# Up-projection of a streaming-encoder block by seven half-size products instead of eight (one level of Strassen's scheme), one core

## The reference, cut to what matters

```python
def conv_gated_mlp(h, w_up, conv_w, conv_b, w_down):      # h (2048, 1024), w_up (1024, 5632)
    z = causal_depthwise_conv(h @ w_up, conv_w, conv_b)   # 3 taps along the tokens, per column
    g, val = jnp.split(z, 2, axis=-1)                     # 2816 gate columns, 2816 value columns
    return (jax.nn.gelu(g, approximate=False) * val) @ w_down
```

## Time and profile before

| | us |
|---|---|
| median of 3 runs (1 core) | 2282.29 |
| lowest, highest | 2281.48, 2282.68 |
| span of the profiled execution | 2280.0 |
| input projection, 0 to 369 | 369.0 |
| mixer, 369 to 791.4 | 422.4 |
| up-projection, 791.4 to 1768.5 | 977.1 |
| down-projection, 1768.5 to 2280 | 511.5 |

### The profile page before, as it was taken

One profiled execution on the slowest core, in us unless ns is written; L12 is line 12 of the kernel. 1 busy time (PEld: TensorE's weight loads), 2 busy tenths in 40 slices (PEclk: granted clock), 3 DMA queues, 4 the chain that ended last, 5 costly groups with the idle time before them and its releaser, 6 DMA issues. The chain is left out here.

```text
span 2280.0 us, 25840 instructions
## 1 busy us (share of the span) xinstructions
PE 2111.2 (93%) x9568; PEld 1717.9 (75%) x9568; DVE 1169.0 (51%) x1238; ACT 632.4 (28%) x912; POOL 481.3 (21%) x317
## 2 busy tenths in 40 slices
PE   4999995789889599999999999999999799999997
PEld 3788884566666378888888888888887588888886
DVE  8698983688888444434424334334344311144333
ACT  4555552344444232221121121121121300031110
POOL 5488773243443200000000000000000000002333
PEclk9999997799999799999999999999999899999999
DMA  6310125223333242112111111111210622342220
GB/s 236 138 43 35 60 74 163 64 91 108 98 100 103 96 149 74 37 37 74 37 37 58 53 37 41 70 37 37 74 37 35 224 76 87 115 134 86 76 87 37
DMA packets 125599, 185.54 MB, mean 81 GB/s; under 512 B 7361, under 2 KB 90305, under 8 KB 122305
## 3 DMA queue, kind: packets, MB, share of 16 engines
q1 hardware_dynamic: 99616, 149.31, 20.1%
q10 hardware_dynamic: 25952, 35.86, 4.4%
HBM read 117.90 MB, written 67.24 MB: 81 GB/s over the span
## 5 line engine op out<-in xcount | busy, mean ns | idle before, releaser
L1387 PE MATMUL u_mm<-u_hT_hi,u_w_hi 128*128 128x512 f32 x1408 | 549.1, 390 | 15.4 <-DVE u_hT_lo L1355 15.4
L1387 PE MATMUL u_mm<-u_hT_lo,u_w_hi 128*128 128x512 f32 x1408 | 548.8, 390 | 0.0
L1387 PE MATMUL u_mm<-u_hT_hi,u_w_lo 128*128 128x512 f32 x1408 | 548.7, 390 | 0.0
L1501 POOL TENSOR_TENSOR d_total<-d_total,d_g 128x1024 f32 x16 | 38.2, 2387 | 1406.1 <-DVE d_total L1588 1406.1
L1321 DVE TENSOR_SCALAR u_y<-u_z,u_taps,u_bias 128x2048 f32<-128x2048 f32 x43 | 57.9, 1347 | 529.9 <-ACT u_z L1269 529.9
L1387 PEld LDWEIGHTS u_mm<-u_hT_hi,u_w_hi 128*128 128x128 f32 x1408 | 265.0, 188 | 70.6 <-DVE u_hT_lo L1355 15.8
L1269 ACT COPY u_z<-u_mm 128x512 f32<-128x512 f32 x176 | 103.2, 587 | 748.8 <-PE u_mm L1387 748.8
L1387 PEld LDWEIGHTS u_mm<-u_hT_hi,u_w_lo 128*128 128x128 f32 x1408 | 265.1, 188 | 55.2
L1387 PEld LDWEIGHTS u_mm<-u_hT_lo,u_w_hi 128*128 128x128 f32 x1408 | 265.1, 188 | 55.1
L1625 PE MATMUL d_y<-d_wd_hi,d_a_hi 128*128 128x512 f32 x704 | 218.9, 392 | 20.7 <-DVE d_wd_lo L1560 20.5
L1625 PE MATMUL d_y<-d_wd_hi,d_a_lo 128*128 128x512 f32 x704 | 217.8, 390 | 0.0
(11 more groups left out here) (172 smaller groups left out, 2506.9 us busy)
## 6 DMA issues: line engine op xcount, KB each, us to landing
u_w_raw<-w_up SPq DMA_DIRECT2D x44, 512.0 KB, 5.8
d_a_raw<-gated_scr SPq DMA_DIRECT2D x32, 704.0 KB, 5.3
gated_scr<-u_y SPq DMA_DIRECT2D x21, 1024.0 KB, 4.6
d_wd_raw<-w_down SPq DMA_DIRECT2D x22, 512.0 KB, 4.7
a_xs<-x SPq DMA_DIRECT2D x16, 512.0 KB, 4.7
m_h_in<-h_scr SPq DMA_DIRECT2D x16, 512.0 KB, 3.4
h_scr<-m_r ACTq DMA_DIRECT2D x16, 512.0 KB, 4.0
h1T_scr<-m_h1T ACTq DMA_DIRECT2D x16, 512.0 KB, 4.4
```

The lines of the kernel that those rows point to most:

```text
L1387: last = nc.tensor.matmul(mm[m][n][:], w[:, m, k, :], h[:, k, bass.ts(n, BLK)], start=(k == 0 and w is w_hi and h is hT_hi), stop=(k == KT ...
L1501: nc.gpsimd.tensor_tensor(tile_of(t), tile_of(t), g_bc[:], ALU.mult).then_inc(scaled_ok, 1)
```

## The change

Three things change in `phase_up`.

**Seven products for eight.** The activations are taken as a 2 x 2 matrix of blocks, by feature half (tiles 0 to 3, tiles 4 to 7) and by token half, the weights of a pair as a 2 x 2 matrix by column tile (gate, value) and feature half. Winograd's form of the scheme gets the four output blocks from seven products of half-size operands, named P1 to P7. Four of the seven weight operands are sums of blocks (`w_sum`: 128x512 each, made by POOL for every pair as `sum1` to `sum4`), four of the seven activation operands are sums too (`t1` to `t4`, once a pass, DVE and POOL). Each operand of a product, 7 on either side, is split into `hi` and `lo` as before. The products are 4 x 3 matmuls of 128x512. P2 is added to P1 in bank 0, P4 to P7 in bank 2, P3 to P5 in bank 3; DVE forms the sums `u2 = P1 + P6`, `u3 = u2 + P7`, and from them the blocks c22, c21 and c12, each from one tile in SBUF and one bank in PSUM (128x512); c11 is P1 + P2, copied by ACT. P4 waits until u3 has read bank 2, P3 until c22 has read bank 3.

**Two passes.** Tokens go in two passes of 1024 with all 22 pairs in each: 44 steps of 7 products. The weights are loaded twice (1 MB for a pair). The last two columns of `z` of each pair are kept in `edge` for the second pass. The activation operands have one set of buffers, which the second pass overwrites in the steps `turn` (21) and `again` (22).

**Moved work.** The first tap with the bias goes from DVE (`tensor_scalar`) to ACT (`activation` Identity with scale and bias), over 1024 columns; the product of gelu and value goes to POOL, except in the last step. Banks are read by DVE, where before ACT copied them all. The last step is no longer cut into pieces of 512 tokens.

In `phase_project` the allocations are closed before its end and its semaphores are cleared by POOL, since the new phase needs more of them.

The core of the diff:

```diff
@@ phase_project
+        ctx.pop_all().close()
+        nums = sorted(s.num for s in used)
+        assert nums == list(range(nums[0], nums[-1] + 1))
+        nc.gpsimd.sem_clear(range(nums[0], nums[-1] + 1))
@@
+P1, P6, P7, P5, P4, P3, P2 = range(7)
+STD = (P1, P6, P7, P5, P4, P3, P2)
+OPEN0 = (P1, P2, P5, P6, P7, P3, P4)
+OPEN1 = (P1, P5, P6, P7, P3, P2, P4)
+BANK = {P1: 0, P2: 0, P6: 1, P7: 2, P4: 2, P5: 3, P3: 3}
+FRESH = (P1, P6, P7, P5)
@@ phase_up: PE
+            def product(st, s, order, fresh):
+                pe.wait_ge(wlo_ok, 7 * st.i + STD.index(s) + 1)
+                if fresh is not None:
+                    pe.wait_ge(rlo_ok, 7 * fresh + RLO[fresh].index(s) + 1)
+                if s in FRESH and not (isinstance(st.i, int) and st.i < 2):
+                    pe.wait_ge({P1: c11_ok, P6: u2_ok, P7: c21_ok, P5: c12_ok}[s], st.i - 1)
+                if s not in FRESH:
+                    pe.wait_ge({P2: p1_ok, P4: u3_ok, P3: c22_ok}[s], st.i + 1)
+                for k in range(HK):
+                    for w, h in ((w_hi, r_hi), (w_hi, r_lo), (w_lo, r_hi)):
+                        last = nc.tensor.matmul(mm[st.slot][BANK[s]][:], w[:, s, k, :], h[:, s, k, :],
...
+                last.then_inc(mm_ok, 1)
@@ phase_up: DVE
+            def make_u3(st, order):
+                dve.wait_ge(mm_ok, made(st, order, P7))
+                dve.wait_ge(u2_ok, st.i + 1)
+                nc.vector.tensor_tensor(u3[:], u2[:], mm[st.slot][2][:], ALU.add).then_inc(u3_ok, 1)
...
+            def step(st):
+                nxt = st.plus(1)
+                if st.p:
+                    pad(st)
+                make_u2(st, STD)
+                weights_lo(nxt, P1)
+                weights_lo(nxt, P6)
+                make_u3(st, STD)
+                weights_lo(nxt, P7)
+                make_c22(st, STD)
+                weights_lo(nxt, P5)
+                make_c21(st, STD)
+                weights_lo(nxt, P4)
+                convolve(st, 1)
+                make_c12(st, STD)
+                weights_lo(nxt, P3)
+                weights_lo(nxt, P2)
+                convolve(st, 0)
+                if not st.p:
+                    keep_edge(st)
@@ phase_up: POOL
+            def sum1(st):
+                pool.wait_ge(w_ld[st.slot], 16 * st.half + 16)
+                if not (isinstance(st.i, int) and st.i == 0):
+                    pool.wait_ge(wlo_ok, 7 * st.i - 7 + P3 + 1)
+                nc.gpsimd.tensor_tensor(w_sum[:, 0, :, :], w_raw[:, st.slot, 1, 0:HK, :], raw_of(st, P4), ALU.add).then_inc(s_ok, 1)
...
+            def gate(st):
+                pool.wait_ge(gelu_ok, st.i + 1)
+                pool.wait_ge(convv_ok, st.i + 1)
+                nc.gpsimd.tensor_tensor(y[:, 1, :], y[:, 1, :], y[:, 0, :], ALU.mult).then_inc(act_ok, 1)
...
+            def step(st):
+                gate(st.plus(-1))
+                sum4(st.plus(1))
+                sums(st.plus(2))
@@ phase_up: ACT
+            def step(st):
+                nxt = st.plus(1)
+                keep_p1(st, STD)
+                weights_hi(nxt, P1, STD)
+                gelu(st.plus(-1))
+                for s in (P6, P7, P5, P4):
+                    weights_hi(nxt, s, STD)
+                tap_v(st)
+                weights_hi(nxt, P3, STD)
+                take_c11(st, STD)
+                weights_hi(nxt, P2, STD)
+                tap_g(st)
@@ phase_up: SP
+            def step(st):
+                refill(st, st.j + 2)
+                store(st.plus(-1))
@@ phase_up: the first step of a pass, DVE
+            def first(st):
+                nxt = st.plus(1)
+                weights_lo(st, P1)
+                right_lo(0, P1)
+                for s in (P6, P7, P5):
+                    weights_lo(st, s)
+                right_lo(0, P2)
+                weights_lo(st, P4)
...
+                nc.vector.tensor_tensor(stage[:, 1, :, :], stage[:, 1, :, :], stage[:, 0, :, :], ALU.subtract).then_inc(t1_ok, 1)
+                weights_lo(st, P3)
+                weights_lo(st, P2)
+                right_lo(0, P5)
+                right_lo(0, P3)
+                right_t2(0)
...
+                right_lo(0, P6)
+                right_lo(0, P7)
+                make_u2(st, OPEN0)
+                weights_lo(nxt, P1)
+                right_lo(0, P4)
+                make_u3(st, OPEN0)
```

More of the change, by code:

```diff
@@ new lines, in steps @@
+        def steps(eng, step, first, turn, again, final):
+            first(Step(0, 0, 0))
+            step(Step(0, 1, 0))
+            with eng.Fori(1, FT // 2 - 1) as n:
+                step(Step(n, 0, 0))
+                step(Step(n, 1, 0))
+            step(Step(FT // 2 - 1, 0, 0))
+            turn(Step(FT // 2 - 1, 1, 0))
+            again(Step(FT // 2, 0, 1))
+            with eng.Fori(FT // 2, FT - 1) as n:
+                step(Step(n, 1, 1))
+                step(Step(n, 2, 1))
+            final(Step(FT - 1, 1, 1))
@@ L1243, in store @@
[L1243 to L1251, removed]
@@ new lines, in penultimate, with turn, again, final @@
+            def penultimate(st):
+                step(st)
+            def turn(st):
+                refill(st, 1)
+                store(st.plus(-1))
+                sp.wait_ge(rlo_ok, 7 + RLO[1].index(P5) + 1)
+                sp.wait_ge(t2_ok, 2)
+                load_b(stage[:, 1, :, :], 1, 1, 0, b21_ld)
+            def again(st):
+                refill(st, 2)
+                store(Step(FT // 2 - 1, 1, 0))
+            def final(st):
+                store(st.plus(-1))
+                store(st)
+                sp.wait_ge(act_st, 16 * 2 * FT)
@@ new lines, in _ @@
+            first(Step(0, 0, 0))
+            step(Step(0, 1, 0))
+            with sp.Fori(1, FT // 2 - 1) as n:
+                step(Step(n, 0, 0))
+                step(Step(n, 1, 0))
+            refill(Step(FT // 2 - 1, 0, 0), 0)
+            store(Step(FT // 2 - 2, 1, 0))
+            turn(Step(FT // 2 - 1, 1, 0))
+            again(Step(FT // 2, 0, 1))
+            with sp.Fori(FT // 2, FT - 2) as n:
+                step(Step(n, 1, 1))
+                step(Step(n, 2, 1))
+            step(Step(FT - 2, 1, 1))
@@ new lines, in final @@
+            def final(st):
+                gate(st.plus(-1))
+            first(Step(0, 0, 0))
+            step(Step(0, 1, 0))
+            with pool.Fori(1, FT // 2 - 1) as n:
+                step(Step(n, 0, 0))
+                step(Step(n, 1, 0))
+            step(Step(FT // 2 - 1, 0, 0))
+            turn(Step(FT // 2 - 1, 1, 0))
+            again(Step(FT // 2, 0, 1))
+            with pool.Fori(FT // 2, FT - 2) as n:
+                step(Step(n, 1, 1))
+                step(Step(n, 2, 1))
@@ new lines, in take_c11, with tap_last @@
+            def take_c11(st, order):
+                act.wait_ge(mm_ok, made(st, order, P2))
+                nc.scalar.copy(z[:, 0, PAD:PAD + BLK], mm[st.slot][0][:]).then_inc(c11_ok, 1)
+            def tap_last(st, m):
+                s = bass.ds(2 * st.j + m, 1)
+                nc.scalar.activation(y[:, m, :], z[:, m, PAD:], ACT.Identity, bias=bias[:, s],
+                                     scale=taps[:, s, PAD:PAD + 1].rearrange("p o t -> p (o t)")).then_inc(tapv_ok if m else tapg_ok, 1)
@@ L1410, in phase_down, with step, first, again @@
+            def step(st):
+                for s in STD:
+                    product(st, s, STD, None)
+            def first(st):
+                for s in OPEN0:
+                    product(st, s, OPEN0, 0)
+            def again(st):
+                for s in OPEN1:
+                    product(st, s, OPEN1, 1)
+            steps(pe, step, first, step, again, step)
 def phase_down(nc, w_down, ln_g, ln_b, act_scr, h1_scr, out):
```

487 lines of the change are left out of this document (335 added, 152 removed).

## The result

The changed kernel takes 2317.41 us (median of 4 runs, 2314.94 to 2319.28) where the kernel before takes 2282.07 on the same chip (4 runs, 2281.48 to 2282.68): 1.0154 times as long, interval 1.0139 to 1.0168. It is slower by 35 us; forecast were 13 us less. The profiled executions span 2312.8 and 2280.0 us.

A forecast was written before the change was run, and what follows sets the result against it. PE bounds the up-projection; afterwards steady steps take 20.0 us with the port. Opening, steps, turn and end sum to a phase end of 1755.7 against 1768.5, 12.8 us less: 2269.5 from 2282.29, range 2228 to 2304.

The forecast's parts named there:

- Products removed: PE in the up-projection: 528 fewer matmuls, 3696 left, worth 119.6 us at most; 19.03 us a step.
- The common port: DVE instructions with two SBUF inputs and POOL's SBUF reads exclude each other; four waits, some 4 us a step.
- Rival A: Steady steps: the port hardly binds, POOL falls into DVE's idle; 19.0 to 19.5 us a step, 2204 to 2258; chance 0.20.
- The steady step: One u3 to the next with port waits: 20.0 us, PE standing about 1 us before P4.
- the ring: Loop through DVE, ACT, one product of PE and four waits for POOL, back to the next u3: 20.0 us.
- Rival B: From c21 to the next u3: DVE sets the time, slower from 20.3 us a step; 2281 to 2312, chance 0.31.
- The second pass: Steps after the turn between passes: 20 steps at 20.0 us each, as in the first pass.
- the walk: The engines' queues followed in order from the start of u3 through one steady step, giving 20.0 us.
- The clock: PE's stop of about 1 us a step before P4 is too short to lower its clock.
- Opening, turn and end: Step 0 ends at 848.4; steps 21 to 23 take 24.0, 44.5 and 24.1 us; after the last product 10.6 us.
- Rival C: ACT reloads tables between Identity and Gelu, 1.28 us each: ring above 21, time 2330; chance 0.04 with anything above.
- The range: Whole kernel's time, 2228 to 2304 us, leaving out half of Rival A and the top tenth.

The follow-up runs named there:

- e1: Changed kernel with POOL's gate product replaced by a memset that only writes, in 43 of the 44 steps; 2230.28 us.
- e4: Changed kernel with the product of gelu and value moved from POOL to DVE, directly behind u3, nothing left out; 2233.35 us, 0.9789 of the kernel before.
- e10: e4 with POOL's three 2048-wide subtractions (t4, t1, t3) moved to DVE; 2224.92 us, 0.9753 of the kernel before.
- e11: e10 with the low parts of P6's and P7's activations made ahead of the first pass's last tap sums; 2221.43 us, 0.9737 of the kernel before.
- e6: Changed kernel with taps and bias read at a constant address on ACT and DVE instead of one from the loop's register; 2290.49 us.
- e5: Changed kernel without the 4-column copy at the start of the second pass's steady steps; 2299.69 us.
- e7: Changed kernel with a 4-column copy like the second pass's added to the first pass's steady steps; 2325.89 us.
- e9: e7 with a second such copy and a wait for its end, just ahead of u3 in the first pass; 2338.64 us.

## Why the prediction was wrong

By its own sum, from the phase's start, in us:

| | forecast | measured | |
|---|---|---|---|
| to the end of step 0 | 57.0 | 57.4 | +0.4 |
| step 1 | 24.1 | 26.9 | +2.8 |
| steps 2 to 20 | 380.0 | 391.4 | +11.4 |
| steps 21 to 23 | 92.6 | 96.9 | +4.3 |
| steps 24 to 43 | 400.0 | 428.6 | +28.6 |
| the end | 10.6 | 10.1 | -0.5 |
| phase | 964.3 | 1011.3 | +47.0 |

- **Products removed.** Right: 3696 matmuls, and PE at 19.04 a step as soon as nothing holds it (e1 to e4, e10, e11).
- **The common port.** Right in kind, shown by e1 to e4, down to the places: P6 held by the gate product, P2 and the gate path's tap sums by the weight sums. Rival A needed a port that hardly binds; it was out.
- **The steady step.** This is the term that failed: 20.0 us, measured 20.63. The step of it that was mis-sized is the stretch from c21 to the end of the value tap sums: "tap on ACT 1.24, each with 0.04 to hand over", then 2.5 for the sums. That is 4.5 us, measured 5.19. The handovers are 0.37 to ACT and 0.18 back, and the pair of sums takes 2.71. The 0.04 came from short instructions of the mixing phase, where no address from a register is in play. The dearer price stood in the earlier trace rows, 5.1 us of idle over 34 instructions, or 0.15 between two tap sums whose addresses come from the register; it was taken over for the tap sums and not for ACT's tap:

```profile
L1325 DVEq FUSED_REGOPS  x80: 53/58/64, 872.3 to 1723.4; - x80
```

  e6 removes 0.45 of the 0.63. What it leaves of the stretch is 4.74 for 4.5: ACT's tap 0.17 behind c21, and 1.28 for a tap sum priced at 1.22 (the pair adds up to 2.59 by the prediction's own prices, not to 2.5). At the end of the value tap sums the ring is 0.67 late, and the whole step 0.63; POOL's sums at 1.29 instead of 1.21 and P2's difference, 0.18 after its cast, lie behind that and add nothing on balance. Rival B had the right place and the right deciding point (20.3 us), and the wrong cause of its extra: dearer POOL work and 0.04 on every DVE instruction, and not the tap's address. Its upper end, 2312, was passed too. Over 39 steps the 0.63 are 25 us: by itself this turns 12.8 us less into 12 more.
- **The second pass.** It was priced like the first, 20.0 a step, with "edge" in the walk for about 0.1 us. That fits the copy into `edge` in the first pass, where u2 starts as the tap sums end. In the second pass the copy out of `edge` waits before and after itself, and nothing was put down for that or for what the shift does to the order at the port. e5 shows that this copy of 0.17 us costs 17.7 us (18.0 by the lengths of the phase): about 0.4 a step because it hands the port to DVE just ahead of the gate product, and six half-clock stretches of 1.65 us, 10 us together.
- **The clock.** "PE so stands about 1 us a step before P4; that is too short to lower its clock" rested on rows of 3.70 and 8.68 us, which show nothing of stops in between. For the 1.29 us of the first pass it held, for six of the longer stops of the second (1.77 to 1.81 us of idle) it did not.
- **Opening, turn and end.** Within 7 us of 184: the waits for the 2048-wide subtractions and the half clock behind the long stops were counted. In the turn this is in part luck: steps 21, 22 and 23 were forecast at 24.0, 44.5 and 24.1 us and took 19.7, 50.7 and 26.5, so that errors of 4 and 6 us offset each other. The turn's largest stop, that before P6:

```profile
1310.57 0.77 PE L1786 MATMUL u_mm<-u_r_hi,u_w_hi 128*128 128x512 f32 x1 [20.18 <-issue]
```

- **Rival C.** Out: no table is loaded between 791 and 1800 us, and the first load behind the phase is L1927:

```profile
1800.32 1.28 ACT L1927 ACT_TABLE_LOAD   x1 [4.32 <-PEq L1230]
```

- **The range.** Its upper end of 2304 allowed for 20.8 us a step at most, with no half clock; 20.6 in the first pass and 21.43 in the second (428.6 / 20), with the opening's 3 us, passed it by 13 us. The result lies in the band above 2312, to which the prediction gave 0.04, and not for that band's reason (C).

## What to carry to other kernels

Work moved to a free engine is priced by what it shares with the busy one: here two groups of POOL instructions, each harmless alone, together cost 1.6 us of every 20.6, and moving one of them onto DVE, by far the busier of the two, made the kernel 84 us faster. On a ring that passes several engines, price each handover from a row with the same kind of operand (an address from a register counts for itself), and walk every variant of the loop body: 0.17 us of work in the wrong place cost 17.7. Keep PE's stops short even among dense matmuls: here one of nearly 2 us cost another 1.65 us of clock in more than half of the cases.

## What was not expected of the hardware

- PE's clock fell to its lower level for about 3.4 us behind stops of 1.93 us and more (1.77 us of idle in the row), with dense matmuls before and after: behind 25 of the 42 such stops in the steady steps of the changed kernel, e7 and e9. It never did behind a shorter one, in either pass: 186 in the steady steps of the changed kernel and e5 to e9, the longest 1.92. Which of the longer stops draws it was not settled.
- An instruction of ACT or DVE whose scalar operand is addressed by a register started 0.10 to 0.20 us later after a wait than the same one with a constant address (the changed kernel against e6: 0.20 for ACT's tap, 0.15 and 0.10 for the two tap sums).
- POOL's `memset` of 128x2048 took 1.82 us beside DVE's two-input instructions and delayed none of them (688 ns each); the product it replaced took 2.40 and delayed one by up to 1.8.
- A 4-column copy within SBUF on DVE was held for 4.4 us by a POOL subtraction in e4. In the changed kernel the first copy into `edge` was held for 1.1 us by POOL's sum3 (855.99 to 858.24):

```profile
857.03 1.24 DVE L1646 COPY u_edge<-u_z 128x4 f32<-128x4 f32 x1
```

  Such a copy has one SBUF input, as the tap sums of the earlier trace rows that were not held. The Trainium skill (SBUF — State Buffer, "Who interferes with whom") names copies among the instructions that can enter a mode in which they take both ports; the rows agree, but no run here tested other copies.
